# Edits to the order of work in a three-layer attention kernel on one core: gate piece in five steps, maxima signalled singly, third layer's scores and sums reordered

## The reference

```python
s = jnp.where(smask, jnp.einsum('bghtd,bgtksd->bghtks', qb, k_sel), NEG)
ps = jax.nn.softmax(s.reshape(...), axis=-1).reshape(s.shape)
o_s = jnp.einsum('bghtks,bgtksd->bghtd', ps, v_sel)
...
o = jnp.einsum('bshc,bshcd->bshd', gates, out).reshape(B, S, NSA_Q) * jax.nn.silu(z)
```

```python
z = jnp.einsum('bhqd,bhkd->bhqk', qb, kb) * SB_SCALE
log_1m_beta = jnp.where(mask, -jax.nn.softplus(z), 0.0)
suffix = lax.cumsum(log_1m_beta, axis=3, reverse=True) - log_1m_beta
w = jnp.where(mask, jnp.exp(jax.nn.log_sigmoid(z) + suffix), 0.0)
```

## Time and profile before

| what | us |
|---|---|
| median of 3 runs | 1207.32 |
| lowest and highest of them | 1207.28, 1438.28 |
| the profiled execution | 1207.31 |
| its span in the profile | 1205.6 |
| TensorE, matmuls busy | 1191.3 (99%) |
| VectorE busy | 629.2 (52%) |
| ScalarE busy | 558.7 (46%) |
| GpSimd busy | 412.5 (34%) |

### The profile page before, as it was taken

One profiled execution on the slowest core, in us unless ns is written; L12 is line 12 of the kernel. 1 busy time (PEld: TensorE's weight loads), 2 busy tenths in 40 slices (PEclk: granted clock), 3 DMA queues, 4 the chain that ended last, 5 costly groups with the idle time before them and its releaser, 6 DMA issues.

```text
span 1205.6 us, 19180 instructions
## 1 busy us (share of the span) xinstructions
PE 1191.3 (99%) x7763; PEld 1018.6 (84%) x7763; DVE 629.2 (52%) x1097; ACT 558.7 (46%) x1069; POOL 412.5 (34%) x295
## 2 busy tenths in 40 slices
PE   8999999999999999999999999999999999999998
PEld 7799879998987677788999898878888888888898
DVE  4587644876577477887270435454431851104434
ACT  5534245635522387786454445454534122343234
POOL 2435331110043255552304323332223653443441
PEclk9999999999999999999999999999999999999999
DMA  8325514567466211002223222212221333323321
GB/s 263 105 75 183 161 36 141 175 179 195 105 126 122 43 36 36 2 2 54 71 71 105 70 71 70 62 45 70 72 70 35 105 105 105 101 91 105 105 70 71
DMA packets 131265, 111.76 MB, mean 93 GB/s; under 512 B 38834, under 2 KB 128048, under 8 KB 131184
## 3 DMA queue, kind: packets, MB, share of 16 engines
q1 hardware_dynamic: 129696, 106.92, 30.5%
q10 hardware_dynamic: 1488, 3.71, 1.3%
HBM read 104.85 MB, written 2.10 MB: 89 GB/s over the span
## 4 chain that ended last, share of the span: by engine, by line
PE 93%; DVE 3%; ACT 3%; issue 0%; ACTq 0%; POOL 0%; DVEq 0%
PE banks L1417 43%; PE banks L1406 13%; PE banks L1440 6%; PE banks L1864 3%; PE banks L1507 3%; PE banks L2028 3%; PE banks L1882 3%; PE banks L1845 3%; PE banks L1905 2%; PE banks L1978 2%; PE banks L2042 2%; PE banks L2073 1%; PE banks L1382 1%; PE banks L1577 1%; PE banks L1729 1%; PE banks L1678 1%
## 5 line engine op out<-in xcount | busy, mean ns | idle before, releaser
L671 POOL TENSOR_TENSOR w_lo<-raw,w_hi 128x1024 fp32r<-128x1024 f32 x130 | 321.3, 2493 | 619.4 <-ACT w_hi L774 619.2
L1417 PE MATMUL banks<-act_hi,w_hi 128*128 128x512 f32 x704 | 277.3, 394 | 0.1
L1417 PE MATMUL banks<-act_lo,w_hi 128*128 128x512 f32 x704 | 274.4, 390 | 0.0
L1417 PE MATMUL banks<-act_hi,w_lo 128*128 128x512 f32 x704 | 274.4, 390 | 0.0
L774 ACT ACTIVATE w_hi<-raw 128x1024 fp32r<-128x1024 f32 (+1 forms) x156 | 154.9, 1043 | 124.8 <-PE banks L1417 97.5
L1417 PEld LDWEIGHTS banks<-act_hi,w_hi 128*128 128x128 f32 x704 | 132.3, 188 | 28.4 <-issue 1.3
L1417 PEld LDWEIGHTS banks<-act_lo,w_hi 128*128 128x128 f32 x704 | 132.1, 188 | 28.0
L1417 PEld LDWEIGHTS banks<-act_hi,w_lo 128*128 128x128 f32 x704 | 132.3, 188 | 26.3
L1406 PE MATMUL banks<-w_hi,act_hi 128*128 128x256 f32 x384 | 109.2, 284 | 0.1
L1406 PE MATMUL banks<-w_hi,act_lo 128*128 128x256 f32 x384 | 108.7, 283 | 0.0
L1406 PE MATMUL banks<-w_lo,act_hi 128*128 128x256 f32 x384 | 108.7, 283 | 0.0
(11 more groups left out here) (447 smaller groups left out, 2484.6 us busy)
## 6 DMA issues: line engine op xcount, KB each, us to landing
raw<-w_in SPq DMA_DIRECT2D x32, 1024.0 KB, 5.7
raw<-gla_w_in SPq DMA_DIRECT2D x11, 1024.0 KB, 5.3
raw<-nsa_w_in SPq DMA_DIRECT2D x29, 256.0 KB, 4.4
raw<-nsa_w_in SPq DMA_DIRECT2D x6, 1024.0 KB, 6.4
raw<-gla_w_out SPq DMA_DIRECT2D x4, 1024.0 KB, 6.6
ada_first<-w_ada SPq DMA_DIRECT2D x4, 1024.0 KB, 8.0
raw<-nsa_w_out SPq DMA_DIRECT2D x16, 256.0 KB, 4.9
raw<-w_branch_a SPq DMA_DIRECT2D x4, 1024.0 KB, 5.1
```

Source lines behind the costliest of these rows:

```text
L671: pool.tensor_tensor(w_lo[:, u, k], raw[:, u, k], w_hi[:, u, k].bitcast(F32), ALU.subtract).then_inc(lo_done, 1)
L1417: mm = pe.matmul(b[:], w[:, u, k, m * P:(m + 1) * P], x[:, k, :], start=(k == 0 and n == 0), stop=(k == KT - 1 and n == 2))
```

## The change

The edits are these. The last gate piece is done in five steps of 5, 5, 5, 5 and 4 matmuls, the last in pair 15, and copied by ScalarE in pair 15. The queries of the last tile are rounded in four copies of 256 columns in pairs 16 to 19, and VectorE subtracts in four pieces. The table for silu is loaded behind the second copy of pair 30. The maxima of the two halves are signalled one by one, and each exponential waits for its own; the other waits on that count are doubled. In the third layer the scores of source tile 0 come between those of tile 3, ahead of the masks, and the 36 sum matmuls come in another order.

```diff
-Z_STEPS, Z_SIZE = 4, 6
+Z_STEPS = (6,) * 12 + (5, 5, 5, 5, 4)
...
-        round_keys, round_queries = {1: 0, 2: 1}, {3: 1, 11: 2, 19: 3}
+        round_keys, round_queries = {1: 0, 2: 1}, {3: 1, 11: 2, 16: 3, 17: 3, 18: 3, 19: 3}
...
-                act.wait_ge(s_max, u + 1)
                 for half in range(2):
+                    act.wait_ge(s_max, 2 * u + half + 1)
...
+                    k = slice(2 * (x - 16), 2 * (x - 16) + 2)
                     act.wait_ge(s_full, 32)
+                    act.activation(score_q_odd[:, k], qT[:, k, t * P:(t + 1) * P], ACT.Copy).then_inc(rounded_high, 1)
+                    return
...
+                if x >= NPAIR // 2:
+                    turned_low(x, 1)
                 if x == NPAIR - 2:
                     act.preload_act_table_set("silu_and_others")
-                if x >= NPAIR // 2:
-                    turned_low(x, 1)
...
-                    pe.wait_ge(s_max, u - 1)
+                    pe.wait_ge(s_max, 2 * (u - 1))
                 if t and i == 0 and w == 0:
-                    pe.wait_ge(rounded_low, 2 + 2 * t)
+                    pe.wait_ge(rounded_low, (4, 6, 10)[t - 1])
...
                 for n in range(3):
                     for a in range(2):
+                        score(p, a, 0, n, start=True)
+                    for a in range(2):
                         score(p, a, 3, n, start=False)
                 for st in (1, 3):
                     score_mask(0, st)
...
                 score_mask(1, 2).then_inc(z_full, 1)
-                for n in range(3):
-                    for a in range(2):
-                        score(p, a, 0, n, start=True)
                 score_mask(0, 0)
                 score_mask(1, 0).then_inc(z_full, 1)
 
+            def source_sum(a, st, jt, n, stop=False):
+
+                return pe.matmul(blocks(z_banks, a, st, skip=jt - st), (tri_r if jt == st else minus_r)[:],
+                                 blocks((sp_hi, sp_lo)[n], a, jt), start=False, stop=stop, skip_group_check=True)
+
...
+                for jt in (3, 2):
+                    for n, part in enumerate((sp_hi, sp_lo)):
+                        pe.matmul(both_heads(z_banks, 2, skip=jt - 2), (tri_r if jt == 2 else minus_r)[:],
+                                  both_heads(part, jt), start=False, stop=(jt == 2 and n == 1), skip_group_check=True)
+                        if jt == 2:
+                            for a in range(2):
+                                source_sum(a, 0, 3, n)
+                for a in range(2):
+                    for n in range(2):
+                        source_sum(a, 1, 2, n)
+                        mm = source_sum(a, 0, 2, n)
+                mm.then_inc(tri_full, 1)
+                for a in range(2):
+                    for n in range(2):
+                        source_sum(a, 1, 1, n)
+                        source_sum(a, 3, 3, n, stop=(n == 1))
+                        source_sum(a, 0, 1, n)
+                        mm = source_sum(a, 1, 3, n, stop=(n == 1))
+                mm.then_inc(tri_full, 1)
+                for a in range(2):
+                    for n in range(2):
+                        mm = source_sum(a, 0, 0, n, stop=(n == 1))
+                mm.then_inc(tri_full, 1)
...
-                last.then_inc(s_max, 1)
+                                             wstat[:, u % 4, 0, half:half + 1]).then_inc(s_max, 1)
```

More of the change, by code:

```diff
@@ L434, in z_piece_end @@
         def z_piece_end(x):
-            return (x + 1) // Z_STEPS if (x + 1) % Z_STEPS == Z_STEPS - 1 and x + 1 < 4 * Z_STEPS else None
+            done = sum(Z_STEPS[:x + 2])
+            return done // (3 * KT) - 1 if done % (3 * KT) == 0 and x + 1 < len(Z_STEPS) else None
         def prob_of(u, half, keys):
@@ L1212, in keys_high, with queries_high @@
                 act.activation(score_k[:, w], (ksT, kwT)[w][:], ACT.Copy).then_inc(rounded_high, 1)
-            def queries_high(t):
+            def queries_high(t, x):
                 if t == 3:
+                    k = slice(2 * (x - 16), 2 * (x - 16) + 2)
                     act.wait_ge(s_full, 32)
+                    act.activation(score_q_odd[:, k], qT[:, k, t * P:(t + 1) * P], ACT.Copy).then_inc(rounded_high, 1)
+                    return
                 for half in range(2):
@@ L1238, in _ @@
                 elif x in round_queries:
-                    queries_high(round_queries[x])
+                    queries_high(round_queries[x], x)
                 elif x in round_weights:
@@ L1888, in z_steps @@
             def z_steps(j):
-                q, r = divmod(j, Z_STEPS)
-                if q >= 4:
+                if j >= len(Z_STEPS):
                     return
+                q, first = divmod(sum(Z_STEPS[:j]), 3 * KT)
                 c, m = C_NZ + 2 + q // 2, q % 2
-                if r == 0:
+                if first == 0:
                     if q == 0:
@@ L1899, in z_steps @@
                         pe.wait_ge(bank_free[2 * (before % 2) + (q - 1) % 2], before // 2 + 1)
-                for n in range(Z_SIZE * r, Z_SIZE * (r + 1)):
+                for n in range(first, first + Z_STEPS[j]):
                     k = n // 3
@@ L1906, in z_steps @@
                                    start=(n == 0), stop=(n == 3 * KT - 1))
-                if r == Z_STEPS - 1:
+                if n == 3 * KT - 1:
                     mm.then_inc(bank_full[2 * (c % 2) + m], 1)
@@ L1954, in _ @@
                 if x == NPAIR - 2:
-                    pe.wait_ge(s_max, NUNIT)
+                    pe.wait_ge(s_max, 2 * NUNIT)
                     mod_row(1, 1)
@@ L2480, in unit_max @@
                 for half in range(2):
-                    last = dve.tensor_tensor_reduce(prob_of(u, half, keys), bank[2 * (u % 2) + half][:, 0:keys],
-                                                    key_mask[:, S - keys:S], -1.0, -NEG, ALU.add, ALU.min,
-                                                    wstat[:, u % 4, 0, half:half + 1])
-                last.then_inc(s_max, 1)
+                    dve.tensor_tensor_reduce(prob_of(u, half, keys), bank[2 * (u % 2) + half][:, 0:keys],
+                                             key_mask[:, S - keys:S], -1.0, -NEG, ALU.add, ALU.min,
+                                             wstat[:, u % 4, 0, half:half + 1]).then_inc(s_max, 1)
             def unit_weights(u):
@@ L2533, in keys_low, with queries_low @@
                 dve.tensor_tensor(k_low_part[w][:], kT[:], score_k[:, w].bitcast(F32), ALU.subtract).then_inc(rounded_low, 1)
-            def queries_low(t):
+            def queries_low(t, x):
                 tok = slice(t * P, (t + 1) * P)
+                if t == 3:
+                    k = slice(2 * (x - 16), 2 * (x - 16) + 2)
+                    dve.wait_ge(rounded_high, 6 + x - 16 + 1)
+                    dve.tensor_tensor(q_low_part[:, k, tok], qT[:, k, tok], score_q_odd[:, k].bitcast(F32), ALU.subtract)\
+                        .then_inc(rounded_low, 1)
+                    return
                 for half in range(2):
@@ L2576, in _ @@
                 elif x - 1 in round_queries:
-                    queries_low(round_queries[x - 1])
+                    queries_low(round_queries[x - 1], x - 1)
                 elif x - 1 in round_weights:
```

## The result

The changed kernel takes 1200.89 us (median of 5 runs, 1200.61 to 1201.23) against 1207.32 us: 6.43 us less, a ratio of 0.9946 with a 95% interval of 0.9935 to 0.9957. One execution of the kernel before that took 1438.28 us is left out of the ratio. The change is within 2%, and inside the range of 1198.5 to 1205.8. The forecast was 1202.5 us, a gain of 4.8 us; 1.6 us more came than it had, and the experiments are about where these are from.

What follows compares the result with a forecast made beforehand. TensorE, busy 99% of the span, was taken as the bound, leaving only gaps or a shorter matmul stream. Terms 0.5 + 1.0 + 0.85 + 0.7 + 1.7 + 0 = 4.75 us took 1207.3 to 1202.5 us, range 1198.5 to 1205.8.

Steps and rivals of the forecast that it cites:

- Maxima singly, pairs 3 to 6: Second layer's attention, pairs 3 to 6: signalling each half's maximum returns 0.5 us of 1.39 us lost, bounds 0 and 0.8.
- a loop shorter by 0.2 us per two pairs: Pairs 3 to 6, scores to scores two pairs on: two interleaved loops return 0.2 us first, then 0.2 per two pairs.
- Gate step at pair 16: TensorE's 1.12 us gap at pair 16: the last gate piece in five steps gains 1.0 us, bounds 0.3 and 1.12.
- Takes back about 0.5 us: ScalarE before pair 16: the gate copy, moved to pair 15, costs about 0.5 us of the 0.9 us lead.
- Table: ScalarE at pair 30: loading behind the copy puts the load in idle time, 553.6 to 554.9, gaining 0.7 us.
- Scores: Third layer's scores, all ahead of the masks: 0.21 us per head pair, 1.7 us in all, bounds 0 and 2.8.
- Loses both changes: 0.11 + 0.10: Third layer's scores: removes the extra time of the first and last wide pairs next to masks, 0.21 us per head pair.
- hidden narrow matmuls: Third layer's sums: narrow matmuls among wide ones hide their weight loading, 5.6 us more gained, 1196.9 us; chance 0.08.
- a price per change of width: Third layer's sums: each change from narrow to wide costs time, 3.6 us back, 1206.1 us; chance 0.09.
- rival of moved waits: Attention: VectorE or GpSimd replaces ScalarE in the loops; 1.0 of 3.05 us remains, 1204.6 us; chance 0.15.
- the broken overlap: Third layer's scores: the two heads run one after the other, 8.2 us slower, 1210.7 us; chance 0.03.
- A risk that I judged by its old margin: Third layer, even pairs: the first score signal comes 0.7 us later, delaying VectorE's use of bank 0; 1.4 us margin holds.

## Why the prediction was right, and where it was short

The mechanism was right in the main: which waits end, that ScalarE's chain holds TensorE in those pairs, that the sums' order is worth nothing, and that the scores gain by leaving the changes between 64-row and 128-row matmuls. The sizes add up to 4.75 us; the stages gave 6.8, of which the time shows 6.4. Every term but that of the sums was too small, and one gain of 0.46 us was not in the sum. The time lies in the forecast's own range of 1200.5 to 1204.5, but only 0.4 us above its lower end.

*Maxima singly, pairs 3 to 6: 0.5 us forecast, 0.82 measured, and 0.06 and 0.18 in pairs 7 and 0.* The step that failed is "a loop shorter by 0.2 us per two pairs". The distances fall by 0.23, 0.19, 0.18 and 0.22 us, 0.2 in every pair. VectorE's row in pair 4 of the kernel before, just ahead of the maximum of the earlier trace rows, shows why:

```profile
433.98 0.17 DVE L2490 RECIPROCAL wstat<-wstat 128x2 f32<-128x2 f32 x1 [0.79 <-ACT prob_small L1172]
```

VectorE waits for the exponentials of one unit before it takes the maxima of the next, and ScalarE waits for these. The chain passes through the signal once per pair, so twice in my loop of two. That is read from the rows; the experiments show the size and that the signal alone brings it. The measured 0.82 us is the forecast's upper bound of 0.8.

*Small waits: not in the sum, 0.46 us measured.* In pairs 23 and 25 to 28 a pair took 0.1 us longer than it does with the single signal, with no wait in the list. Maxima singly, alone, removes it; the rows put it down to ScalarE's copy being late.

*Gate step at pair 16: 1.0 forecast, 1.11 measured.* "Takes back about 0.5 us" was wrong: alone the step gives 0.86, and the signal adds 0.25 where the forecast had 0.5. That the sum came near is luck: the copy's price was set 0.5 too high and the signal's share 0.25 too high, and the gap of 1.12 us caps both.

*Queries: 0.85 forecast, 0.87 measured.* That the single signal covers the pieces is shown: without it they cost 0.12 us a pair.

*Table: 0.7 forecast, 0.89 measured.* I took the listed idle time of 0.68 us for the wait's price. By starts it is more: the value matmul that waited starts 0.95 us after the one before it, where 0.10 us is usual, since the one before still counts as busy for 0.27 us, and the next comes 0.05 us late. With this edit alone the load ran from 554.22 to 555.50, behind the whole copy, not from 553.6 as the forecast has it; the 1.00 us behind it covers that.

*Scores: 1.7 forecast, 2.4 measured.* "Loses both changes: 0.11 + 0.10" named the right cause with too few places. The 0.10 us of the last wide pair stays; what goes instead are 0.10 at the narrow pairs ahead of the masks and 0.09 between the masks and the first wide pair. The masks' place is worth 0.25 us, and the mixing, costed at nothing, gives 0.05.

*Sums: 0 forecast, 0.02 us a head pair lost.* The price of 0.111 us per narrow matmul stands wherever it is. The rivals of hidden narrow matmuls (1196.9) and of a price per change of width (1206.1) both fall with the sums alone, since the sums take 5.33 us and not 4.6 or 5.8. The Trainium skill ("TensorE: Matmul & The Clock Gate", section Step-by-step: what each phase is for) says that weight loads are pulled ahead of running matmuls; the 5.33 us speak against more than one of them being pulled ahead here.

The rival of moved waits (1204.6) falls: no new wait stands in the list. So does that of the broken overlap (1210.7): the scores take 2.64 us, and the two heads' matmuls start together for wide and narrow alike. A risk that I judged by its old margin is closer than it looked. VectorE's use of bank 0 in head pair 4, after, and ScalarE's taking of the product's second half:

```profile
798.92 0.68 DVE L2647 SCALAR_TENSOR_TENSOR br_hi<-banks,qh 128x512 fp32r<-128x512 f32 x1
...
800.16 0.60 ACT L1263 ACTIVATE qh<-banks 128x512 fp32r<-128x512 f32 x1 [3.71 <-PE banks L1421]
```

VectorE is done at 799.60, 0.56 us ahead of ScalarE's start on that half. Before, the same distance was 805.70 - 803.44 - 0.68 = 1.58 us, and the forecast gave it a loss of 0.7 us; it was 1.0. The 0.3 us by which the scores became shorter may be the rest, since the product ends earlier by them; no run takes that apart.

What stays open is why TensorE's wait for `xn_tok` near 10 us varies from one execution to the next, by which the first gate step starts up to 0.6 us later in some profiles, and whether tasks cut to half size, rather than moved, would free pairs 3 to 6. Neither was tried.

## What to carry to other kernels

In a chain of engines that hand small pieces to each other, signal each piece when it is done. Where two engines wait for each other in turn, the saving counts once per turn, and it makes room for other edits that need slack. Measure a stage by the distance between equal instructions of neighbouring iterations: waits of 0.1 us appear in no list of idle time, and listed ones cost more than they show. Group matmuls by the rows that they use. Their order by width is worth little in itself: 0.05 us a head pair for the scores, nothing for the sums.

## What had not been expected of the hardware

A change between 64-row and 128-row matmuls costs about 0.12 us each: two fewer per head pair gave 0.25 us net of what the new order of widths costs or saves. It is spread over the matmuls on both sides, so that no single row shows it whole. It stands where all operands are f32, too: the first pair of 64-row scores behind the second layer's turning takes 0.28 us instead of 0.17. Mixing narrow 64-row pairs between wide ones gave 0.05 us a head pair, while mixing 128-row narrow matmuls between wide ones gave nothing (5.33 against 5.31 us); the runs do not show why the two differ.
